# Tokens held in TensorE for the down-projection, and the closing norm inside the last block

## The reference

```python
x = layer_norm(ALPHA * x + h @ w_out, ln1_g, ln1_b)
u = jax.nn.relu(x @ w_up)
return layer_norm(ALPHA * x + (u * u) @ w_down, ln2_g, ln2_b)
```

## Time and profile before

| | us |
|---|---|
| median of three runs | 2963.66 |
| lowest and highest run | 2951.36, 2967.2 |
| span of the profiled execution | 2953.3 |
| TensorE busy in it | 2803.1 |
| VectorE busy | 1887.3 |
| ScalarE busy | 842.9 |
| GpSimd busy | 207.3 |

### The profile page before, as it was taken

One profiled execution on the slowest core, in us unless ns is written; L12 is line 12 of the kernel. 1 busy time (PEld: TensorE's weight loads), 2 busy tenths in 40 slices (PEclk: granted clock), 3 DMA queues, 4 the chain that ended last, 5 costly groups with the idle time before them and its releaser, 6 DMA issues. The chain is left out here.

```text
span 2953.3 us, 58897 instructions
## 1 busy us (share of the span) xinstructions
PE 2803.1 (95%) x25775; PEld 2658.4 (90%) x25775; DVE 1887.3 (64%) x2204; ACT 842.9 (29%) x1226; POOL 207.3 (7%) x226
## 2 busy tenths in 40 slices
PE   7999999999999887899899999999999999999995
PEld 7998889888887665899789999999999999999994
DVE  3264555455553685536877777777777777777775
ACT  2221222122212355213533233232232322322321
POOL 2011101110110321001000000000000000000003
PEclk9999999999999899999999999999999999999997
DMA  9489999999999722445122232332323323323222
GB/s 343 154 314 402 410 374 412 411 400 394 413 396 340 246 79 82 104 132 138 51 79 86 86 114 71 103 106 67 115 84 88 109 72 107 101 71 115 79 94 89
DMA packets 340851, 548.62 MB, mean 186 GB/s; under 512 B 20940, under 2 KB 244781, under 8 KB 330019
## 3 DMA queue, kind: packets, MB, share of 16 engines
q1 hardware_dynamic: 263682, 334.37, 34.0%
q0 software_dynamic: 13872, 141.28, 11.8%
q10 hardware_dynamic: 63040, 69.21, 6.9%
HBM read 508.96 MB, written 35.84 MB: 184 GB/s over the span
## 5 line engine op out<-in xcount | busy, mean ns | idle before, releaser
L2129 DVE SCALAR_TENSOR_TENSOR base<-big_G,base 128x544 f32<-128x544 f32 x512 | 369.6, 722 | 244.3 <-PE big_G L1964 244.3
L449 PE MATMUL prj_G<-prj_xh,prj_wh 128*128 128x280 f32 x1696 | 504.0, 297 | 20.8 <-DVE prj_wl L692 13.9
L451 PE MATMUL prj_G<-prj_xh,prj_wl 128*128 128x280 f32 x1696 | 498.5, 294 | 0.0
L450 PE MATMUL prj_G<-prj_xl,prj_wh 128*128 128x280 f32 x1696 | 497.8, 294 | 0.0
L699 DVE STREAM_TRANSPOSE prj_kT<-base 128x4096 f32<-128x4096 f32 x64 | 284.5, 4445 | 258.3 <-PE prj_S L482 258.3
L2041 ACT ACTIVATE wh<-raw 128x1024 fp32r<-128x1024 f32 x227 | 239.4, 1059 | 652.8 <-PE big_G L1964 542.8
L1962 PE MATMUL big_G<-ff_uh,wh 128*128 128x272 f32 x1360 | 392.3, 288 | 3.6 <-DVE base L2129 3.5
L1963 PE MATMUL big_G<-ff_ul,wh 128*128 128x272 f32 x1360 | 393.5, 289 | 0.0
L1964 PE MATMUL big_G<-ff_uh,wl 128*128 128x272 f32 x1360 | 393.4, 289 | 0.0
L449 PEld LDWEIGHTS prj_G<-prj_xh,prj_wh 128*128 128x128 f32 x1696 | 322.9, 190 | 46.3 <-issue 34.5
L2116 DVE TENSOR_TENSOR wl<-raw,wh 128x1024 fp32r<-128x1024 f32 x227 | 277.0, 1220 | 86.3 <-ACT wh L2041 86.3
(11 more groups left out here) (418 smaller groups left out, 6097.2 us busy)
## 6 DMA issues: line engine op xcount, KB each, us to landing
prj_v_nat<-in_cache_v SPq DMA_DIRECT2D x242, 512.0 KB, 7.6
raw<-in_w_down SPq DMA_DIRECT2D x128, 512.0 KB, 4.4
raw<-in_w_up SPq DMA_DIRECT2D x120, 512.0 KB, 4.4
prj_raw<-in_w_in ACTq DMA_DIRECT2D x103, 512.0 KB, 17.6
raw<-in_w_out SPq DMA_DIRECT2D x16, 1024.0 KB, 7.1
prj_scratch<-prj_stage ACTq DMA_DIRECT2D x53, 280.0 KB, 9.3
out_xr<-x_scratch SPq DMA_DIRECT2D x16, 544.0 KB, 4.0
base<-in_cache_v SPq DMA_DIRECT2D x14, 512.0 KB, 7.2
```

What stands on the lines that cost most here:

```text
L449: mm(out, w_hi[:, k, m], xh[:, k0 + k, cols], start=(first and k == 0), stop=False)
L450: mm(out, w_hi[:, k, m], xl[:, k0 + k, cols], start=False, stop=False)
L451: last = mm(out, w_lo[:, k, m], xh[:, k0 + k, cols], start=False, stop=(end and k == nk - 1))
L2129: V.scalar_tensor_tensor(out, G[2 + t % 2][:, :, 0:HALF_M], 1.0 / ALPHA, out, ALU.mult, ALU.add).then_inc(y_done, 1)
```

## The change

- **Down part.** Token tiles of 128 from uh and ul are stationary, and 512 columns of w_down stream (`wide`). The result lies with tokens on partitions in `acc`, [128 tokens, 4 tiles, 2048], in `base`. A unit is two banks (1024 columns; one bank in block 0), in PAIR = [G[2], G[1]] by turns, so G[1] is now used by up and down parts: `down` waits for the last `accumulate`, and product 2 of the up part for the last `add`.
- **Samples.** Their 32 tokens are taken out (`us`, copied by ScalarE in `u_high`) and multiplied in `sample` by plain fp32 matmuls with the raw weights, in four column groups of one bank that gathers over all 32 blocks. SyncE's `load_up` waits for it, as it reads `raw`.
- **x1.** `phase_out` writes x1 into a new tensor `parts` (two ScalarE instructions for each tile), `turn_back` turns it on TensorE into the token layout in block 0 (64 transposes) and ScalarE copies it to `acc` (`take_back`). T1 to T4 replace parts of `parts` in place (`sums`), in a new order. GpSimd keeps the samples' x1 in `x1s`.
- **Last block and closing norm.** `down_last` goes token tile by token tile with all four pieces present. `sum_samples` gathers the samples' four banks and their x1 after tile 1. The norm runs inside `phase_ff` in the order 0, 1, samples, 2, 3; `phase_end` is gone. The last tile is normalised, scaled and offset in four pieces of 512 columns, offset by VectorE, and stored in four.

```diff
+            def wide(out, t, w_hi, w_lo):
+                at = tokens(t)
+                for k in range(FB):
+                    mm(out, uh[:, k, at], w_hi[:, k, :], start=(k == 0), stop=False)
+                    mm(out, ul[:, k, at], w_hi[:, k, :], start=False, stop=False)
+                    last = mm(out, uh[:, k, at], w_lo[:, k, :], start=False, stop=(k == FB - 1))
+                return last
+            def sample(b):
+                for d in range(DOWN):
+                    pe.wait_ge(raw_full[BY_FREE[d]], 16 * down_fill(b))
+                for k in range(FB):
+                    for d in range(DOWN):
+                        last = mm(SAMPLE[NS * d:NS * (d + 1), :], us[:, k, :], down_raw(d)[:, k, :],
+                                  start=(b == 0 and k == 0), stop=(b == LAST_BLK and k == FB - 1))
+                last.then_inc(sample_ps, 1)
-            def down(b, base, phase, first=False):
+            def down(b, base):
+                pe.wait_ge(low_done, NLOW + b)
+                pe.wait_ge(added, 6 * b + 6)
                 for d in range(DOWN):
                     pe.wait_ge(lo_done, base + d + 1)
-                    for i in range(4):
-                        t = 4 * d + i
-                        if not (first and t < 2):
-                            pe.wait_ge(y_done, KT * b + t - 1)
-                        for c, cols in enumerate(HALVES):
-                            for k in range(FB):
-                                last = third(G[2 + t % 2][:, c, 0:HALF_M], w_hi[:, k, i * P:(i + 1) * P], w_lo[:, k, i * P:(i + 1) * P],
-                                             uh[:, k, cols], ul[:, k, cols], k == 0, k == FB - 1)
+                    for pair in range(2):
+                        v = 2 * d + pair
+                        pe.wait_ge(y_done, first_unit(b) + (v - 1 if b > 1 or v > 0 else 0))
+                        for t in (2 * pair, 2 * pair + 1):
+                            last = wide(PAIR[v % 2][:, t % 2, :], t, w_hi, w_lo)
                         last.then_inc(down_ps, 1)
+                    if d == 0:
+                        sample(b)
...
+            def down_last(base):
+                pe.wait_ge(low_done, NLOW + LAST_BLK)
+                sample(LAST_BLK)
+                slots = [(ring_h[(base + d) % RING], ring_l[(base + d) % RING]) for d in range(RING)] + [(fourth_h, fourth_l)]
+                for t in range(NT):
+                    for half in range(2):
+                        v = 2 * t + half
+                        pe.wait_ge(y_done, first_unit(LAST_BLK) + v - 1)
+                        for d in (2 * half, 2 * half + 1):
+                            pe.wait_ge(lo_done, base + d + 1)
+                            w_hi, w_lo = halves_of(slots[d])
+                            last = wide(PAIR[v % 2][:, d % 2, :], t, w_hi, w_lo)
+                        last.then_inc(down_ps, 1)
+                    if t == 1:
+                        sum_samples()
...
                 for d in range(DOWN):
                     sp.wait_ge(lo_done, base - DOWN + d + 1)
+                    sp.wait_ge(sample_ps, b)
                     load_up(BY_FREE[d], b + 1)
...
             def u_high(b, downs=None):
+                for k in range(FB):
+                    A(two(us[:, k, :]), sample_columns(two(u2[:, k, :])), ACT.Copy)
                 A(uh[:, :, :], u2, ACT.Copy).then_inc(uh_done, 1)
...
+            def turn_back(kp):
+                if kp > 0:
+                    pe.wait_ge(back_done, NT * kp)
+                for t in range(NT):
+                    for n in range(4):
+                        x = part(2 * (n // 2) + t // 2, kp)[:, n % 2, P * (t % 2):P * (t % 2 + 1)]
+                        last = tr(TURNED[t][:, n * P:(n + 1) * P], x, ident[:, :])
+                    last.then_inc(back_ps, 1)
...
+            def add(b, v):
+                dv.wait_ge(down_ps, first_unit(b) + v + 1)
+                out = unit_out(b, v)
+                V.scalar_tensor_tensor(out, PAIR[v % 2][:, :, :], 1.0 / ALPHA, out, ALU.mult, ALU.add).then_inc(y_done, 1)
...
+            for i, t in enumerate(CLOSING):
+                if t == "samples":
+                    dv.wait_ge(rows_ps, 1)
+                    for d in range(DOWN):
+                        ins = V.bn_stats(stats[0:r, d, :], ROWS[d])
+                else:
+                    add(b, 2 * t)
+                    add(b, 2 * t + 1)
+                    for d in range(DOWN):
+                        dv.wait_ge(y_done, first_unit(b) + 2 * t + d // 2 + 1)
+                        ins = V.bn_stats(stats[:, d, :], acc[:, t, WIDE * d:WIDE * (d + 1)])
...
+                if i > 0:
+                    finish(i - 1)
+            for d, cols in enumerate(QUARTERS):
+                dv.wait_ge(sd_norm, NORM_AT[-1] + d)
+                V.tensor_tensor(acc[:, t, cols], acc[:, t, cols], gain[:, cols], ALU.mult).then_inc(moments_scale_gain, 1)
+                dv.wait_ge(moments_scale_gain, LAST_GAIN_AT + 2 * d)
+                V.tensor_tensor(acc[:, t, cols], acc[:, t, cols], offset[:, cols], ALU.add).then_inc(moments_scale_gain, 1)
```

More of the change, by code:

```diff
@@ L2015, in _, with sum_samples @@
+            def sum_samples():
+                pe.wait_ge(rows_done, 1)
+                for d in range(DOWN):
+                    mm(ROWS[d], ident[:, NS * d:NS * (d + 1)], rows, start=True, stop=False)
+                    for k in range(4):
+                        last = mm(ROWS[d][:, k * P:(k + 1) * P], x1s[:, 4 * d + k, :], ident[:, :], start=False, stop=(k == 3))
+                last.then_inc(rows_ps, 1)
             up_plain()
-            down(0, DOWN, DOWN, True)
+            down_first()
@@ L2029, in _, with high_to @@
             A = nc.scalar.activation
-            def high(slot, q, fills=0, ups=None, downs=None, sums=None):
-                if not (isinstance(fills, int) and fills == 0):
+            def high_to(out, q, fills=0, ups=None, downs=None, after=None):
+                if fills:
                     ac.wait_ge(raw_full[q], 16 * fills)
@@ new lines, in _ @@
+            turn_low(T1, t1, 1, 8)
+            for kp in (2, 3):
+                n = 4 * kp
+                difference(t0, 3, 1, kp, n)
+                second(t1, t0, kp, n + 1, n + 1)
+                turn_low(T3, t0, kp, n + 1)
+                fourth(t0, t1, kp, n + 2, n + 2)
+                turn_low(T2, t1, kp, n + 2)
+                low(2 + kp, BY_FREE[kp - 2])
+                difference(t1, 1, 0, kp, n + 3)
+                turn_low(T4, t0, kp, n + 3)
+                turn_low(T1, t1, kp, n + 4)
@@ new lines, in _, with finish @@
+            for b in range(1, LAST_BLK):
+                ff_block(b)
+            b, base = LAST_BLK, FIRST + NCH * (NBLK - 2)
+            add(b - 1, 4)
+            low(base, 0)
+            add(b - 1, 5)
+            add(b - 1, 6)
+            low(base + 1, 2)
+            add(b - 1, 7)
+            u_low(b)
+            low(base + 2, 1)
+            low_to(fourth_l, base + 3, fourth_h, 3)
+            step = Chain(dv, dve)
+            def finish(i):
+                t = CLOSING[i]
+                o = out_s if t == "samples" else acc[:, t, :]
+                dv.wait_ge(small_in, 32)
+                dv.wait_ge(sd_norm, NORM_AT[i])
+                V.tensor_tensor(o, o, gain[0:(NS if t == "samples" else P), :], ALU.mult).then_inc(moments_scale_gain, 1)
@@ L2334, in _ @@
[L2334 to L2350 removed]
+                    .then_inc(moments_scale_gain, 1)
```

584 lines of the change are left out of this document (330 added, 254 removed).

## The result

The changed kernel takes 2975.18 us (median of 5 runs, 2969.06 to 2979.12), the one before 2959.47 (5 runs, 2951.36 to 2967.2; three of them are the ones ahead of the prediction). The ratio is 1.0049, with a 95% interval of 1.0028 to 1.007: slower by half a per cent, where 0.9% less was forecast. 2975.18 lies just beyond the upper end of the range.

A forecast was written before the change was run, and what follows sets the result against it. TensorE, busy for 95% of the span, was taken as the bound. Block 0 -2, blocks 1 to 30 -9 and the closing -15.3 made -26 us: 2937 us beside 2963.66 (0.9% less), range 2917 to 2975.

The forecast's parts named there:

- Wide matmuls: Down part: 96 matmuls of 512 columns at 216.5 ns, 20.8 us in place of 24.16, a gain of 3.4 us a block.
- proportional: 237 ns: Upper bound of the 512-column step, surplus growing with the columns: a gain of only 1.4 us a block.
- the slower rival: Down part: streaming 512 single-pass columns is bound by reading, 237 ns, +1.7 us a block, 2998 us; chance 0.07.
- fixed surplus: Down part: 226 ns a wide matmul, blocks +18 us, in all 2964, no change; chance 0.20.
- The new wait: Start of `down`: TensorE waits for the up part's last `accumulate`, 0.85 us a block, not below 0.5.
- Samples: `sample` in the down part: plain fp32 matmuls in four overlapping column groups, 2.0 us a block with changing over.
- The up turn: Start of `up`: two small ScalarE copies before uh make VectorE's u_low later, 0.2 us a block.
- The clock: Sign: clock at 1.00 through blocks 1 to 30; the rival that pauses lower it gave 2988 us, chance 0.04.
- Block 0: First block: one wait of some 3 us in place of three, 57.4 against 59.8 us; net -2, from -6 to +8.
- The closing: Last block and norm, bound by VectorE: 61.5 us in place of 76.8, so -15.3; -20 to -10 by meshing.
- held to 30: Closing: GpSimd's offset holds VectorE's scale of the samples until 30 us after the last matmul of block 30.
- held to 53.5: Closing: GpSimd's offset of tile 2 holds VectorE to 53.5 us, before the other seven quarter operations.

The follow-up runs named there:

- in-phase kernel: Changed kernel with uh and ul in rows of 256 columns, without sample columns, so stationary slices begin where weight slots do modulo 256 bytes: 2961.78 us, ratio 1.0008.
- its control: The in-phase kernel with sixteen unused columns ahead of uh, moving uh and ul by 64 bytes: 2972.46 us.
- the first run: No kernel: streams of matmuls in otherwise empty programs, by width, type and neighbours; 512 fp32r columns settled at 226.7 ns, bf16 at 215.8.
- both experiments on it: Changed kernel with the wait moved to the second unit: 2949.13 us, ratio 0.997; kernel before with that wait added: 2984.04 us, ratio 1.0091.

## Why the prediction was wrong

**Wide matmuls: the step that failed.** "I take 216.5, as at 512 columns whatever shares the time with a matmul has twice the time to hide." It measured 232.7: 16.2 ns x 96 x 30 = 47 us, the whole miss of 44 us in these blocks and a little more. The bound "proportional: 237 ns" was nearest. The prediction lets the slower rival decide "from 229 ns on (2979)"; that working is off, since by its own sum 229 ns gives 2973 and 2979 needs 231.2. The measured step is past either. The time, 2975, lies between that rival's 2998 and the 2964 of the fixed surplus, as the true step lies between theirs. Two parts make the 16.2 ns. (1) 5 to 6 ns are the start addresses, shown by the in-phase kernel and its control (227.6 and 233.3 ns). (2) The other 10 to 11 are there in phase too, and alone: 226.7 ns, which is the "fixed surplus" rival's 226. Why an fp32r matmul of 512 columns takes 13.3 ns over its columns, where bf16 has 2.5, stays open. My error was to lean on the plain fp32 row of 0.43 us: plain passes are another form, and the first run has 429.2 ns for one beside 226.7 for fp32r: their surplus of 2.5 ns says nothing about fp32r's 13.3. The rows at 272 and 280 columns were the only ones of the right form, and their slope, (128.4 - 125.8) / 8 = 0.33 ns a column, was too rough to tell fixed from proportional.

The Trainium skill, "TensorE: Matmul & The Clock Gate", section "Back-to-back issue gap", gives columns / 2.4 + 2.5 ns. For 512 columns that is 215.8 ns. The first run agrees for bf16 (215.8) and contradicts it for fp32r (226.7).

**The new wait: right.** 0.85 us a block was forecast. The pause is 0.81 as a mean over the thirty (0.94 from start to start less 0.13), and 0.1 for the slower second matmul makes 0.91; the longest was 1.79 from start to start. It is 25 to 26 us by both experiments on it. With it even a step of 227.6 ns is no gain: the in-phase kernel stands at 1.0008. The prediction took it as given by G[1], though only unit 1 needs it.

**Samples: right.** 1.95 us against 2.0; the four column groups overlap, four matmuls in 0.43 us a pass. The measure for it was miscounted: behind 3.45 us stand 16 rounds of 128 columns and 8 of 256, not "16 rounds of single passes (215.8 ns each)". The sum is the same.

**The up turn: right.** 0.2 us was forecast. The step ahead of product 4 is 0.41 us (1570.21 to 1570.61 is one) where the kernel before has 0.22:

```profile
2068.72 0.29 PE L1964 MATMUL big_G<-ff_th,big_wl 128*128 128x272 f32 x1
2068.94 0.39 PE L1962 MATMUL big_G<-big_xh,wh 128*128 128x272 f32 x1
```

Yet the up part is only 0.06 us longer (21.43 against 21.37 us), since its other steps went from a mean of 126.0 to 125.3 ns, 0.12 us in all. The prediction had nothing on that, and its cause is open.

**The clock: right.** 1.00 through blocks 1 to 30, after pauses of 0.7 to 1.7 us; it fell only behind longer ones: 3.50 us in block 0, and 3.8 and 2.4 before and in block 31.

**Block 0: off by 2.3 us.** One wait near 3 us was forecast, and 3.50 came, followed by slow clock (a mean of 0.97), which the sum had left out.

**The closing: right, step by step.** 61.5 us forecast and measured, and each step of VectorE's chain within 0.9 us. The samples' scale "held to 30" ended at 2943.6 - 2913.0 = 30.6; VectorE "held to 53.5" was held to 54.0. That GpSimd's offset holds VectorE's two-input operations is shown by the 4.87 us row, and by the edit that takes it away; it is the rule of the Trainium skill, "SBUF — State Buffer", section "Who interferes with whom", and this trace agrees.

The sample round and the new wait miss by about 0.05 us a block each, one under and one over. Sum: +47 (wide step), -4 (other steps of the up part), +2 (block 0), +1 (outside the change) make 46 of the 47 us between forecast and measured span. (The lower end of the range, 2917, is 2920 by the terms that the prediction gives for it.)

## What to carry to other kernels

A change that pays by the width of its matmuls needs the step of that form, type and width; where the trace has none, the middle of the bounds is a better forecast than the hopeful one. Here it was 226.5 ns, 10 ns more, and would have said "no change"; even that was 6 ns short. When long streams of fp32r have 512 columns, let stationary and moving slices begin at the same place modulo 256 bytes: rows of 272 columns broke this, rows of 256 cost nothing and gave 13 us in the changed kernel. No run here shows a gain from it at 256 or 272 columns. And place a wait at the first instruction that needs it, not at the head of its phase: one unit later, it was worth 25 us.

## What the runs showed of the hardware

- The time of an fp32r matmul of 512 columns depends on where its operands begin. At the same place modulo 256 bytes in each partition it took 226.7 to 227.3 ns alone and 227.6 in the kernel; with all or half of the stationary operands 64 or 128 bytes off, 230.1 to 233.4 ns alone and 233.3 in the kernel. The rule isn't whole: 32 stationary columns took 231.7 with both operands at the same place, and one and the same pair of places took 230.1 in one program and 232.5 in another.
- At fewer columns no cost of the place shows. 256 columns took 120.0 ns at the same place, 120.0 with all operands 96 bytes apart (first run), 118.3 with half of them 64 apart, and 116.5 in the kernel with three in four apart. 272 columns took 126.7 at 96 bytes apart and 125.8 in the kernel before.
- In the first run the settled means from 256 to 512 columns are multiples of 6.67 ns (18, 19, 19, 26, 31 and 34 of them): 272 and 280 columns take the same 126.7.
- The first fp32r matmul after another form or a pause is followed 0.1 us late by the second: 0.34 us from start to start behind the sample round of the in-phase kernel, where 0.227 is usual.
- GpSimd's 128 x 2048 add made a VectorE add with two inputs in SBUF take 4.87 us in place of 0.69, but two of VectorE's adds of 1024 columns with one input in PSUM ran beside such an add in 2.33 us together; one alone took 1.22.
